# Two output-projection tiles placed between the steps of the last head's triangular solve

## The reference, cut to what matters

```python
    sol = lax.linalg.triangular_solve(A, rhs, left_side=True, lower=True, unit_diagonal=True)
...
    S_T, o = lax.scan(step, S0.astype(f32), xs)
...
    mix = jnp.concatenate([out_lru, out_dn], axis=-1) @ p['w_out']
...
    x = x + g1[:, None] * mix
```

## Time and profile before

| | us |
|---|---|
| median of three timed runs | 4422.45 |
| lowest and highest of them | 4420.88, 4426.56 |
| the profiled execution's own time | 4424.48 |
| its span, first to last instruction | 4422.7 |
| PE busy, PEld busy | 3754.4, 3491.1 |
| DVE busy, POOL busy, ACT busy | 3025.6, 2101.4, 1477.9 |

### The profile page before, as it was taken

One profiled execution on the slowest core, in us unless ns is written; L12 is line 12 of the kernel. 1 busy time (PEld: TensorE's weight loads), 2 busy tenths in 40 slices (PEclk: granted clock), 3 DMA queues, 4 the chain that ended last, 5 costly groups with the idle time before them and its releaser, 6 DMA issues. The chain is left out here.

```text
span 4422.7 us, 65816 instructions
## 1 busy us (share of the span) xinstructions
PE 3754.4 (85%) x24298; PEld 3491.1 (79%) x24298; DVE 3025.6 (68%) x4531; ACT 1477.9 (33%) x1891; POOL 2101.4 (48%) x1162
## 2 busy tenths in 40 slices
PE   6777999999996898987678989988888888888887
PEld 3337888898885797987578988888888888888886
DVE  5777644555554213897967877776778888888886
ACT  5664343443442113223333333232222222222222
POOL 2432222212224133324356767666666667676672
PEclk9998999999997898998889999999999999999998
DMA  8981212222212122223389999999999999999994
GB/s 308 358 314 64 78 64 82 77 77 73 75 67 68 60 98 108 81 70 111 137 315 386 402 395 408 393 384 366 364 381 380 386 401 387 390 395 392 408 403 157
DMA packets 253130, 1090.63 MB, mean 247 GB/s; under 512 B 25352, under 2 KB 78856, under 8 KB 172296
## 3 DMA queue, kind: packets, MB, share of 16 engines
q1 hardware_dynamic: 167440, 543.60, 32.9%
q0 software_dynamic: 73728, 536.90, 29.9%
q10 hardware_dynamic: 11776, 7.52, 0.5%
HBM read 1047.54 MB, written 40.40 MB: 246 GB/s over the span
## 5 line engine op out<-in xcount | busy, mean ns | idle before, releaser
L248 POOL TENSOR_TENSOR wlo<-raw,whi 128x1024 fp32r<-128x1024 f32 x551 | 1343.1, 2441 | 1495.4 <-ACT whi L244 1487.6
L244 ACT CAST whi<-raw 128x1024 fp32r<-128x1024 f32 x672 | 698.8, 1049 | 1284.7 <-DMA raw<-in_u 535.5
L263 PE MATMUL gps<-hi_d,whi 128*128 128x320 f32 x2048 | 661.6, 323 | 168.3 <-POOL wlo L248 116.1
L2096 PE MATMUL gps<-chi,whi 128*128 128x320 f32 x2048 | 653.8, 319 | 124.7 <-DVE outacc L2225 82.0
L263 PE MATMUL gps<-lo_d,whi 128*128 128x320 f32 x2048 | 651.7, 318 | 0.0
L263 PE MATMUL gps<-hi_d,wlo 128*128 128x320 f32 x2048 | 650.6, 318 | 0.0
L2096 PE MATMUL gps<-clo,whi 128*128 128x320 f32 x2048 | 643.2, 314 | 0.0
L2096 PE MATMUL gps<-chi,wlo 128*128 128x320 f32 x2048 | 643.1, 314 | 0.0
L2183 DVE SCALAR_TENSOR_TENSOR dps<-ring,coef,dps 128x2048 f32<-128x2048 f32 x252 | 591.8, 2348 | 7.6 <-DMA ring<-in_v_rows,spi 3.1
L2170 DVE CUSTOM_DVE_ANT_0 ring<-ring,dps 128x2048 f32<-128x2048 f32 x256 | 582.2, 2279 | 0.0
L263 PEld LDWEIGHTS gps<-hi_d,whi 128*128 128x128 f32 x2048 | 402.1, 196 | 186.7 <-POOL wlo L248 126.4
(11 more groups left out here) (388 smaller groups left out, 6064.6 us busy)
## 6 DMA issues: line engine op xcount, KB each, us to landing
raw<-in_u SPq DMA_DIRECT2D x256, 512.0 KB
raw<-in_v SPq DMA_DIRECT2D x256, 512.0 KB
wada<-in_w_ada SPq DMA_DIRECT2D x96, 1024.0 KB, 6.4
raw<-in_w_in SPq DMA_DIRECT2D x96, 512.0 KB
gateD<-gst SPq DMA_DIRECT2D x8, 2560.0 KB, 7.5
gate<-gateD SPq DMA_DIRECT2D x32, 640.0 KB
raw<-in_w_out SPq DMA_DIRECT2D x32, 512.0 KB
raw<-in_w_q SPq DMA_DIRECT2D x32, 512.0 KB
```

The lines of the kernel that those rows point to most:

```text
L244: act.copy(whi[:, k.slot, :], raw_of(k)).then_inc(W.hi, 1)
L248: pool.tensor_tensor(wlo[:, k.slot, :], raw_of(k), whi[:, k.slot, :].bitcast(F32), ALU.subtract).then_inc(W.lo, 1)
L263: m = pe.matmul(gps[:, bank, 0:DT], w, x[:, kt, :], start=(kt == 0 and n == 0), stop=(kt == KT - 1 and n == 2))
L2096: m = pe.matmul(gps[:, 2 + dt, 0:DT], w[:, slot, cols], x[:, buf, c, :], start=(c == 0 and n == 0), stop=(c == NG - 1 and n == 2))
```

## The change

Halves 0 and 1 of w_out are loaded before SP's wait for w_in and before `mixin`, and POOL rounds them before the fifteen slices. Halves 2 and 3 are loaded after `mixin` and rounded by POOL after the slices; in the output block SP, ScalarE and POOL no longer do them. In `body(None, 7)` TensorE calls `out_ahead(e - 14)` at the start of slots 14 to 29. The calls 0 to 7 are tile 0 and the calls 8 to 15 tile 1; a call does two slices (twelve matmuls), the last of each tile one (six), 180 matmuls in all. In the output block one slice, kt = 15, is left of each of the two tiles. A half is counted as used where its last slice is done, and both halves of tile 1 are counted at its end.

```diff
-        def gemm_part(pe, k, half, pair, first, count, ready=None, parts=whole_halves):
+        def gemm_part(pe, k, half, pair, first, count, ready=None, parts=whole_halves, used=1):
...
-            if first + count == 8:
-                m.then_inc(W.used, 1)
+            if first + count == 8 and used:
+                m.then_inc(W.used, used)
...
+                    for n in range(2):
+                        load_half(sp, a["w_out"][n], Nth(N4 + n))
                     sp.wait_ge(W.used, N4)
...
-                    for n in range(2):
+                    for n in range(2, 4):
                         load_half(sp, a["w_out"][n], Nth(N4 + n))
...
+                    def w_out_half(n):
+                        k = Nth(N4 + n)
+                        pool.wait_ge(w_loaded[raw_at(k)], loads(k))
+                        pool.wait_ge(W.used, k.n - 3)
+                        pool.tensor_copy(whi[:, k.slot, :], raw_of(k)).then_inc(W.hi, 1)
+                        split_lo(pool, k)
+
+                    for n in range(2):
+                        w_out_half(n)
                     for k in range(KT - 1):
...
+                    for n in range(2, 4):
+                        w_out_half(n)
...
+                    def mixed(pe, kt):
+                        pe.wait_ge(S.mixlo, kt + 1)
+
+                    def out_ahead(n):
+
+                        m, kt = n // 8, n % 8 * 2
+                        if n % 8 == 0:
+                            pe.wait_ge((S.evv, S.evz)[m], H)
+                        gemm_part(pe, Nth(N4 + 2 * m + kt // 8), kt // 8, m, kt % 8, min(2, KT - 1 - kt), mixed,
+                                  used=1 - m)
+
                     def body(h, g, ch):
...
+                            if not A and 14 <= e < 30:
+                                out_ahead(e - 14)
...
-                    for n in range(2, 4):
-                        load_half(sp, a["w_out"][n], Nth(N4 + n))
...
-                    for j in (2, 3):
-                        split_hi(act, Nth(N4 + j))
...
-                    for j in (2, 3):
-                        split_lo(pool, Nth(N4 + j))
...
-                    tile(0, Nth(N4), 0)
-                    tile(1, Nth(N4 + 2), 1)
+                    for m in range(2):
+                        gemm_part(pe, Nth(N4 + 2 * m + 1), 1, m, 7, 1, used=1 + m)
```

## The result

| | before | after |
|---|---|---|
| median, us | 4424.51 (4 runs) | 4376.69 (4 runs) |
| lowest and highest | 4420.88, 4432.38 | 4368.83, 4383.3 |
| profiled execution, its span | 4424.48, 4422.7 | 4374.36, 4372.5 |

The ratio is 0.9882 (95% interval 0.9859 to 0.9905). Lines behind the edit are 14 to 20 higher after: L899, L912, L922 are now L919, L932, L942.

What follows compares the result with a forecast made beforehand. TensorE bounds the output block; the last head's levels are a chain with 14.3 us of TensorE holes. -5.5 and -17.8 make -23.3 us: 4424.5 to 4401.2, less 2.0 for the median, 4399.2; range 4395 to 4404 (chance 0.70).

Steps and rivals of the forecast that it cites:

- Nothing behind the output block is tied to a time of its own: Code behind the output block: no gain or loss of its own added to the sum of -23.3 us.
- Levels: Last head's levels: end at 1460.2 instead of 1465.7, -5.5 us, though 180 matmuls were added.
- The scan behind the levels: Last head behind slot 30: no filler there, so unchanged, block's end 23.3 us later as before.
- The clock: TensorE in the last head's levels: slow clock of 0.50 for 5.4 us, then 1.00 to the end of level 6.
- a clock that stays low: Rival, last head's levels: clock stays 0.50, fillers cost +30.7 us, kernel 12.9 us slower, 4435.4; chance 0.05.
- a late clock: Rival, last head's levels: clock rises one or two levels late, 6 to 12 us lost, 4405 to 4411; chance 0.10.
- unshortened levels: Rival, last head: holes filled but levels keep their length, 0 for -5.5 us, 4404.7; chance 0.06.
- POOL's new work: Before `mixin`: POOL rounds two halves of w_out, some 3.4 us each, where otherwise idle; `mixin` not later.
- 38 was the mark: Sign of error: `mixin` issued less than 38 us before the end of L899, 38.5 in the kernel before.
- Output block: Start of the output block: DVE takes up tile 2 after about 24 us instead of 42, -17.8 us.
- The weights of halves 5 to 7: Rival, output block's new start: loads of w_out bind, halves 5 and 6 late, 6 us lost, 4405; chance 0.06.
- the forecast 23.3: Whole gain forecast: -5.5 in the levels and -17.8 in the output block, -23.3 us.

Runs made afterwards that it cites:

- experiment 5: Changed kernel less four TensorE instructions (waits that others cover), so the PEER loops lie as in the kernel before; ratio 0.9949 to the kernel before.
- experiment 9: Kernel before plus 76 TensorE instructions (152 already met waits) ahead of the PEER groups, first loop at the end of a block; ratio 1.0011.
- experiment 3: Kernel before plus 140 TensorE instructions ahead of the PEER loops; 4405.62 us, ratio 0.9926.
- experiment 1: Kernel before plus four TensorE instructions (eight already met waits) ahead of the PEER loops; 4394.68 us, ratio 0.989.
- experiment 6: Kernel before plus 179 TensorE instructions, part in the last head, part ahead of the PEER groups, third loop at a block's end; ratio 0.9971.
- experiment 7: Changed kernel with only tile 0 ahead (slots 14 to 21), tile 1 whole in the output block; ratio 0.9885 to the kernel before.
- experiment 4: Changed kernel with the moved matmuls' sums thrown away, both tiles done whole in the output block, 148 instructions restoring loop places; ratio 0.9972 to the kernel before.
- experiment 2: Changed kernel plus sixteen TensorE instructions (32 waits) ahead of the PEER loops; ratio 0.9874 to the kernel before.

## Why the prediction was wrong

**The step that failed** is the last sentence of the sum, "Nothing behind the output block is tied to a time of its own". It puts what the change does to the code behind it at nothing. That code does not hang on the change's time, but it does on its length: four TensorE instructions more moved the second PEER loop out of the last places of a block. That was worth the 26.3 us of the second loop in the traces, and about 0.7% by the ratios (0.9882 and 0.986 against 0.9949 in experiment 5). That the kernel before lay so that four instructions cured it was luck. With the loops held, the same work gave the forecast (experiment 5), and with a loop shifted into the last places of a block the kernel before lost all that the second loop had shed (experiment 9).

**The terms of the sum held,** save one that was put at nothing and may not be:
- *Levels*, forecast -5.5, measured 52.7 to 48.0, -4.8 before rounding. Level 1 took 1426.51 - 1417.34 = 9.2 us (9.3 forecast), levels 2 to 6 38.8 (38.0).
- *The scan behind the levels* was counted as unchanged. It took 23.3 us before and 22.3 after, but the clock that it gets is not always that of this one execution. In the other four traces of kernels without fillers it took 23.0 and 23.3 us (experiments 3 and 9) and 28.7 twice (1 and 6), and 28.7 in experiment 7, whose fillers end at slot 21. In all seven traces with fillers up to slot 29 it took 22.3 to 23.4. The whole stretch of the scan in the trace before, in experiment 1 and in the trace after:

```profile
1465.70:1489.00 23.30, 10.55 (x52) 7.20 (x52) 5.58 (x12) 7.25 (x12) 0.00 (x0) 0.79 0.13 39
1467.00:1495.70 28.70, 16.61 (x53) 11.96 (x51) 5.58 (x12) 7.25 (x12) 0.00 (x0) 0.50 0.10 31
1465.30:1487.60 22.30, 9.50 (x53) 6.68 (x51) 5.58 (x12) 7.25 (x12) 0.00 (x0) 0.84 0.13 40
```

  The same work at a clock of 0.50 throughout is 5.4 us longer. Fillers may so be worth 1 to 6 us here as well, a term that the sum put at nothing. These thirteen traces point to it and don't prove it, since three of five kernels without fillers had the fast clock anyway; this pair of traces has 1.0 of it.
- *The clock.* Forecast at 0.50 for 5.4 us and then 1.00; it rose within the 6 us shown and stayed. The rivals of a clock that stays low, of a late clock and of unshortened levels fell.
- *POOL's new work.* The two halves are rounded from 1352.4 to 1360.8 and `mixin` is issued at 1378.54, 38.8 us before the end of L919 (38 was the mark). No wait for POOL stands between the levels.
- *Output block*, forecast -17.8, measured 42.1 to 24.9 = -17.2. Tile 2 starts 9.7 us behind the block's start (9.2 forecast): POOL's subtraction started 6.9 us behind the block's start, as forecast, and took 2.77 us where I had 2.4. From there to VectorE 15.14 us (15.1 forecast).
- *The weights of halves 5 to 7* did not bind: the last residual starts at 1709.8 before and 1691.2 after, 18.6 us earlier, although the sample products ran 4.4 us later after (1409.34 and 1413.77). Counted from them, 23.0 us of the forecast 23.3 are there at the block's end. The 4.4 us are no cost of the change: the first DeltaNet head is already 7 us later (497.5 and 504.6), before any edited part has run, and the traces of the kernels without fillers have that head from 495.9 to 504.7.

With the loops held in place the whole change measures 0.9949 (experiment 5). Tile 0 and the fillers alone (7 and 4) agree with the parts in the trace.

**What stays open.** Four instructions gave the kernel before 1.1% (0.8 to 1.4), 35 us at the least, where its second loop has 26.2 us of waits and, by the pace of experiment 9, some 6 of slow clock behind them (28, 29 and 24 matmuls in the 6 us behind the three returns, at clocks of 0.64, 0.67 and 0.56). The lower end nearly fits, the middle (49 us) doesn't, and I have no second place to name; the profiled execution of experiment 1 was the slowest of its four (4415.14 us), so its trace cannot show one. Nor is it shown why the fetches at a return are not begun earlier, or why a loop over eight blocks is fetched anew at all. The 128 KB that the Trainium skill gives for TensorE ("Advanced Engine Details and Errata", section "ISA Cache") would hold eight lines of 16 KB; the packets show that such a loop did not stay loaded here.

## What to carry to other kernels

An edit that adds or drops a few instructions ahead of a long hot loop can move its time by more than the edit itself: before a gain or loss is ascribed to the moved work, compare the count of instruction packets and the waits on "issue" at the loops' returns in the two profiles, and measure the edit once with the loops held in place. A loop over more blocks than stay loaded does little harm where another wait stands at its return, and most where its first instruction is among the last of a block. In a chain that alternates between engines, independent matmuls that close the gaps can cost less than nothing, as they keep the clock up for the short ones: here 180 of them, and the levels took 48 us in place of 52.7.

## What the runs showed of the hardware

- An instruction packet is 16 KB. In the nine returns of experiments 2 and 3 one packet starts in the stop, and TensorE stood still for 3.6 to 4.0 us. In the twelve of the kernel before and experiments 4, 5 and 9 two start, and it stood still for 7.9 to 9.6. Where two stops are seen apart (experiment 6), the second took 4.6 to 5.1. In the stretch shown of experiment 9 the DMA share was 0.98.
- Whether a loop of 1610 instructions was fetched anew in each turn hung on its start: shifts of 0, 4, 76, 140 and 179 instructions of the kernel before gave 132, 105, 132, 159 and 160 packets.
- After 8.8 us without a matmul the granted clock was 0.54 over the next 6.0 us, with TensorE busy throughout, and 1.00 behind them (experiment 9).
- The same scan of one head took 22.3 to 23.4 us in ten traces, at a mean clock of 0.77 to 0.87, and 28.7 in three at 0.50.
- Waits that are already met are not free in number: the wait before the first matmul of the PEER groups was 16.5 us before and with 4 instructions more, 17.5 with 76 more and 24.6 with 140 more.
